# Splitting weights nearer to their use: merge by column chunks, the softmax projections' first weights loaded during the scans, the MLP's split moved inside its turn, the scans' tokens in quarters

## The reference, cut to what matters

```
h = rms_norm(x, norm_mix_g) * (1.0 + sc_m) + sh_m
proj = einsum('bsd,de->bse', h, w_in)            # a_q a_k a_v | b_* | c_* | gates (3 x 1024)
o_a = mixer_diff_attn(a_q, a_k, a_v, ...)        # softmax branch, 4 heads, width 512
o_b = mixer_hgrn2(b_*, ...)                      # gated scan, width 256
o_c = mixer_gla(c_*, ...)                        # gated scan, width 256
g_a, g_b, g_c = split(sigmoid(gates), 3)
merged = g_a * (o_a @ w_up_a) + g_b * (o_b @ w_up_b) + g_c * (o_c @ w_up_c)
x = x + gt_m * (merged @ w_out)
h = rms_norm(x, norm_mlp_g) * (1.0 + sc_f) + sh_f
x = x + gt_f * (square(relu(h @ mlp_w1)) @ mlp_w2)
```

## Time and profile before

| | |
|---|---|
| time, median of 3 runs | 4508.22 us (4507.63 to 4508.64) |
| the profiled execution | 4506.89 us |
| its span, first to last instruction | 4505.1 us |
| mean granted TensorE clock | 0.929 |
| PE busy | 3856.6 us (86%) |
| DVE busy | 2588.6 us (57%) |
| ACT busy | 1651.8 us (37%) |
| POOL busy | 502.5 us (11%) |

### The profile page before, as it was taken

The page is one execution under the profiler, slowest core; times in us unless marked ns, Lnnn a source line. Parts: engine busy times, 40 slices in busy tenths (PEclk is TensorE's granted clock), DMA queues, the critical chain, the costliest instruction groups (busy, mean ns, idle before and its releaser), DMA issues. The chain is left out here.

```text
span 4505.1 us, 56411 instructions
## 1 busy us (share of the span) xinstructions
PE 3856.6 (86%) x22256; PEld 3126.4 (69%) x22256; DVE 2588.6 (57%) x3973; ACT 1651.8 (37%) x2217; POOL 502.5 (11%) x471
## 2 busy tenths in 40 slices
PE   5988998977897999999797999499677798994996
PEld 2766876766676888886697887277566587872774
DVE  6266771159555555555433773587655465745776
ACT  2213331146330000003113773276613465732675
POOL 0001121000000000000131000034102000000341
PEclk9989999989898999999898999699888899996998
DMA  7101112230431111111213103299702302022998
GB/s 296 42 22 61 64 64 96 73 126 22 140 134 66 56 37 56 53 40 69 91 59 142 34 16 137 93 377 371 237 21 81 83 21 110 15 103 94 352 377 277
DMA packets 136489, 518.88 MB, mean 115 GB/s; under 512 B 17952, under 2 KB 70336, under 8 KB 118224
## 3 DMA queue, kind: packets, MB, share of 16 engines
q1 hardware_dynamic: 101936, 411.94, 24.9%
q0 software_dynamic: 31216, 101.85, 7.2%
q10 hardware_dynamic: 3120, 2.10, 0.2%
HBM read 427.21 MB, written 88.62 MB: 115 GB/s over the span
## 5 line engine op out<-in xcount | busy, mean ns | idle before, releaser
L2038 ACT ACTIVATE mlp_relu<-mlp_z 128x512 f32<-128x512 f32 x64 | 38.3, 598 | 641.1 <-PE mlp_z L155 641.1
L3083 DVE TENSOR_TENSOR ring_r<-ring,oN_r 128x4096 fp32r<-128x4096 f32 x48 | 212.2, 4424 | 67.4 <-ACT oN_r L3014 67.4
L153 PE MATMUL scans_G<-ring_r 128*128 128x512 f32 x544 | 221.8, 408 | 32.7 <-ACT scans_stg L2541 18.7
L3083 DVE TENSOR_TENSOR ring_r<-ring,hT_r 128x4096 fp32r<-128x4096 f32 x48 | 212.3, 4423 | 58.0 <-ACT hT_r L3014 58.0
L153 PE MATMUL mlp_z<-ring_r,mlp_w_high_r 128*128 128x512 f32 x512 | 201.3, 393 | 22.0 <-DVE ring_r L147 21.9
L3014 ACT ACTIVATE oN_r<-ring 128x4096 fp32r<-128x4096 f32 x48 | 174.0, 3628 | 84.1 <-DMA ring<-in_w_all 70.0
L154 PE MATMUL mlp_z<-hT_r,mlp_w_high_r 128*128 128x512 f32 x512 | 200.2, 391 | 0.0
L155 PE MATMUL mlp_z<-ring_r 128*128 128x512 f32 x512 | 200.2, 391 | 0.0
L153 PE MATMUL mlp_y_ps<-mlp_w_high_r,oN_r 128*128 128x512 f32 x512 | 199.6, 390 | 0.0
L155 PE MATMUL mlp_y_ps<-mlp_w_high_r,oN_r 128*128 128x512 f32 x512 | 199.2, 389 | 0.0
L154 PE MATMUL mlp_y_ps<-ring_r,oN_r 128*128 128x512 f32 x512 | 199.2, 389 | 0.0
(11 more groups left out here) (643 smaller groups left out, 10661.7 us busy)
## 6 DMA issues: line engine op xcount, KB each, us to landing
ring<-in_w_all SPq DMA_DIRECT2D x118, 2048.0 KB, 10.6
ring<-in_w_mlp SPq DMA_DIRECT2D x16, 2048.0 KB, 7.7
ring<-in_w_all SPq DMA_DIRECT2D x12, 1024.0 KB, 6.3
branch_gates<-scans_stg POOLq DMA_DIRECT2D x48, 256.0 KB, 2.3
merge_raw<-branch_gates SPq DMA_DIRECT2D x16, 768.0 KB, 5.1
ring<-in_w_even SPq DMA_DIRECT2D x6, 1536.0 KB, 8.2
qk_turned<-even_gemm_y POOLq DMA_DIRECT2D x48, 128.0 KB, 2.2
even_qk<-qk_turned SPq DMA_DIRECT2D x6, 1024.0 KB, 5.2
```

What stands on the lines that cost most here:

```text
L153: pe.matmul(out, lh, rh, start=start, stop=False)
L2038: act.activation(r[:, n % 2, :], Z[:, n % 4, :], ACT.Relu).then_inc(z_free, 1)
L3083: dve.tensor_tensor(buf_r[:, b, :], buf[:, b, :], w_high[n % RING].bitcast(F32), ALU.subtract)\
```

## The change

Four edits. In the merge, weights are cast and split by chunk (`ct`), one unit ahead of their use, and the token tiles 4 to 7 are turned, cast and split as 1, 1 and 2 tiles behind units 0, 1 and 2. The v weights of diff_gemm are loaded by SP in the scans, when the tiles of the last load but one are done, under a semaphore of their own (`v_in`), and are cast and split in two halves. The MLP's split of the next W1 follows the add for product 7 instead of 12. The tokens at the start of the scans are cast and split in quarters, and PE waits for quarters 0 and 1, and for 2 and 3.

```diff
@@ merge_stage
-        LATER = {0: (4, 5, 6, 7)}
+        LATER = {0: (4,), 1: (5,), 2: (6, 7)}
+        def chunk(t_, ct):
+            return t_[:, ct // 4, :].rearrange("p (k n) -> p k n", k=KD)[:, :, (ct % 4) * P:(ct % 4 + 1) * P]
 (PE)
-                if th == 0 and ct % 2 == 0:
-                    pe.wait_ge(w_split, half + 1)
+                if th == 0:
+                    pe.wait_ge(w_split, ct + 1)
 (ACT)
-            def cast(half):
-                act.wait_ge(m["up_in"][half], 16)
-                act.activation(w_high[:, half, :], buf[:, half, :], ACT.Copy).then_inc(w_cast, 1)
+            def cast(ct):
+                act.wait_ge(m["up_in"][ct // 4], 16)
+                act.activation(chunk(w_high, ct), chunk(buf, ct), ACT.Copy).then_inc(w_cast, 1)
             cast(0)
-            for t in range(NT):
+            for t in range(HT):
                 take(t)
-            cast(1)
             for g in range(N):
+                if g + 1 < KD:
+                    cast(g + 1)
+                for t in LATER.get(g - 1, ()):
+                    take(t)
 (DVE)
             low_w(0)
-            for t in range(NT):
+            for t in range(HT):
                 low_o(t)
             for g in range(N):
-                if g == 1:
-                    low_w(1)
+                if g + 1 < KD:
+                    low_w(g + 1)
+                for t in LATER.get(g - 1, ()):
+                    low_o(t)
@@ diff_gemm_stage
-            for s_ in range(NS):
+            for s_ in range(1, NS):
...
-                if s_ == 0:
-                    for h in range(4):
-                        sp.dma_start(kn(of(raw, 0))[:, :, h * P:(h + 1) * P], src[h, :, :, 2 * P:3 * P])\
-                          .then_inc(w_in[0], 16)
 (PE)
+                    if n == 0 and k % (KD // 2) == 0:
+                        pe.wait_ge(w_split, 1 + k // (KD // 2))
 (ACT)
-            cast_w(0)
+            act.wait_ge(m["v_in"], 64)
+            for part in range(2):
+                act.activation(half_of(high(0), part), half_of(of(raw, 0), part), ACT.Copy).then_inc(w_cast, 1)
@@ scans_stage (SP, behind the last of its loads)
+            sp.wait_ge(bg_done, last_tile(len(LOADS) - 2))
+            for h in range(4):
+                sp.dma_start(buf[:, 0, :].rearrange("p (k n) -> p k n", k=KD)[:, :, h * P:(h + 1) * P],
+                             m["w_diff"][h, :, :].rearrange("p (k n) -> p k n", k=KD)[:, :, 2 * P:3 * P])\
+                  .then_inc(m["v_in"], 16)
 (PE)
-                    pe.wait_ge(h_split, n + 1)
+                    pe.wait_ge(h_split, 2 * n + 2)
 (ACT; DVE alike)
-            def cast_h(half):
-                toks = slice(half * HALF, (half + 1) * HALF)
+            def cast_h(q):
+                toks = slice(q * 2 * P, (q + 1) * 2 * P)
             cast_h(0)
+            cast_h(1)
             cast_first(0, ready[first % RING], 16 * (first // RING + 1))
-            cast_h(1)
+            cast_h(2)
+            cast_h(3)
@@ mlp_stage (DVE)
-                    if n == NY - 4:
+                    if n == NT - 1:
                         dve.wait_ge(m["mlp_w_in"][0], i * 16 + 32)
                         split(step, dve, buf[:, 0, :], w_high[:, 0, :], buf_r[:, 0, :]).then_inc(w_split, 1)
```

More of the change, by code:

```diff
@@ L1388, in low_o, with low_w @@
                                   o_high[:, :, t * P:(t + 1) * P].bitcast(F32), ALU.subtract).then_inc(o_split, 1)
-            def low_w(half):
-                dve.wait_ge(w_cast, half + 1)
-                dve.tensor_tensor(buf_r[:, half, :], buf[:, half, :], w_high[:, half, :].bitcast(F32), ALU.subtract)\
+            def low_w(ct):
+                dve.wait_ge(w_cast, ct + 1)
+                dve.tensor_tensor(chunk(buf_r, ct), chunk(buf, ct), chunk(w_high, ct).bitcast(F32), ALU.subtract)\
                    .then_inc(w_split, 1)
             low_w(0)
-            for t in range(NT):
+            for t in range(HT):
                 low_o(t)
@@ L1440, in of, with half_of @@
             return slots[s_ % RING][:, 0:KD * WIDE[s_]]
+        def half_of(ap, part):
+            return ap[:, part * SLOT // 2:(part + 1) * SLOT // 2]
         def kn(ap):
@@ L1451, in _ @@
                     sp.wait_ge(done, LAST[s_ - RING])
-                if s_ == 0:
-                    for h in range(4):
-                        sp.dma_start(kn(of(raw, 0))[:, :, h * P:(h + 1) * P], src[h, :, :, 2 * P:3 * P])\
-                          .then_inc(w_in[0], 16)
-                else:
-                    sp.dma_start(kn(of(raw, s_)), src[s_ - 1, :, :, 0:2 * P]).then_inc(w_in[b], 16)
+                sp.dma_start(kn(of(raw, s_)), src[s_ - 1, :, :, 0:2 * P]).then_inc(w_in[b], 16)
         @block.gpsimd
@@ L1475, in _ @@
                 s_ = 0 if n < NT else 1 + (n - NT) // 4
-                if n == 0 or n in LAST:
-                    pe.wait_ge(w_split, s_ + 1)
+                if n in LAST:
+                    pe.wait_ge(w_split, s_ + 2)
                 if n >= 4:
@@ L1494, in cast_w @@
             def cast_w(s_):
-                act.wait_ge(w_in[s_ % RING], 64 if s_ == 0 else 16 + 64 * (s_ == 4))
+                act.wait_ge(w_in[s_ % RING], 16)
                 if s_ >= 2:
@@ L1513, in low_w @@
             def low_w(s_):
-                dve.wait_ge(w_cast, s_ + 1)
+                dve.wait_ge(w_cast, s_ + 2)
                 dve.tensor_tensor(of(low, s_), of(raw, s_), high(s_).bitcast(F32), ALU.subtract).then_inc(w_split, 1)
-            for s_ in range(NS):
+            for part in range(2):
+                dve.wait_ge(w_cast, part + 1)
+                dve.tensor_tensor(half_of(of(low, 0), part), half_of(of(raw, 0), part), half_of(high(0), part).bitcast(F32),
+                                  ALU.subtract).then_inc(w_split, 1)
+            for s_ in range(1, NS):
                 low_w(s_)
@@ L2646, in _, with low_h @@
             step = Steps(dve, stepped)
-            def low_h(half):
-                toks = slice(half * HALF, (half + 1) * HALF)
-                dve.wait_ge(h_cast, half + 1)
+            def low_h(q):
+                toks = slice(q * 2 * P, (q + 1) * 2 * P)
+                dve.wait_ge(h_cast, q + 1)
                 dve.tensor_tensor(h_low[:, :, toks], m["hT"][:, :, toks], h_high[:, :, toks].bitcast(F32), ALU.subtract)\
@@ L2658, in _ @@
             low_h(0)
+            low_h(1)
             low_first(0)
-            low_h(1)
+            low_h(2)
+            low_h(3)
             low_first(1)
@@ L3186, in build_program @@
         m["mlp_w_in"] = [ctx.enter_context(nc.semaphore(f"mlp_w_in{j}")) for j in range(2)]
+        m["v_in"] = ctx.enter_context(nc.semaphore("v_in"))
         m["up_in"] = [ctx.enter_context(nc.semaphore(f"up_in{j}")) for j in range(2)]
```

## The result

| | before | after |
|---|---|---|
| median beside each other, 4 runs each | 4507.93 us (4505.30 to 4508.64) | 4474.88 us (4470.33 to 4478.31) |
| ratio, 95% interval | | 0.9927 (0.9910 to 0.9944) |
| the profiled execution | 4506.89 us | 4474.20 us |
| its span | 4505.1 us | 4472.3 us |
| mean granted TensorE clock | 0.929 | 0.932 |

The change makes the kernel 33.1 us faster; 36.4 had been forecast. In two later comparisons the changed kernel was 38.8 and 40.6 us faster; the intervals of the three ratios overlap.

A forecast was written before the change was run, and what follows sets the result against it. TensorE, busy 86% of the span, was taken as the bound, with gains only from its gaps and slow clock; -13.5 - 20.9 - 1.9 - 0.1 = -36.4 gave 4470.5 profiled, 4471.8 us forecast as median, range 4465 to 4481.

The forecast's parts named there:

- v weights: Start of diff_gemm: weights loaded in the scans lie ready, PE starts at 781.4 instead of 794.90, -13.5 us.
- the halves alone: diff_gemm: if the load still came last, only half a cast and half a subtraction would be saved, -3.9 us.
- merge: start: Merge ahead of unit 0: tile 0 no longer waits for a whole slot's subtraction, -5.7 us.
- merge: unit 0: Merge's first unit: as slow as before, 13 matmuls in 5.64 us; 2.6 us more gained if the clock is up.
- merge: transposes: Merge behind unit 0: the four later tiles, spread, take 3.8 us instead of 5.39, -1.6 us.
- merge: waits, slow stretches: Merge: PE's waits for products go, -9.9 with 0.5 given back; slow stretches of 9 and 12 matmuls go, -4.2 us.
- tokens: Start of the scans: quarters hidden by ACT's wait for the weights' DMA, -0.1 us, between +0.5 and -0.5.
- (1): Merge: gates behind the feed overrun the 0.7 us slack, PE waits again, costing 6.1 us: 4477.9 us; 16%.
- (2): diff_gemm: early v load collides with stores or lands no sooner, -13.5 shrinks to -3.9: 4481.4 us; 3%.
- (3): Merge: the clock is up in unit 0 as well: 4469.2 us; 25%.
- (4): Merge: DVE reads 8-piece chunks slowly; sign turns from 5.7 us a chunk, 13.9 slower: 4522.1 us; 1%.
- (5): Merge: alternating casts and sigmoids on ACT load tables, 1.28 us twice a unit: 4475 us; 2%.

The follow-up runs named there:

- experiment 3: Kernel before with v weights cast and subtracted in halves, but loaded at diff_gemm's start as before: 4503.15 us, ratio 0.9981.
- experiment 5: Kernel before with only the tokens cast and split in quarters: 4505.11 us in one run.
- experiment 8: Kernel before with the ring's 4 MB feed issued behind the merge's second gate load instead of its third: 4506.89 us against 4506.40.
- experiments 1: Kernel before with the v weights' part alone, loaded in the scans and cast and subtracted in halves: 4494.57 us against 4509.16, ratio 0.9965.

## Why the prediction was right, step by step

| term | forecast | measured in the traces |
|---|---|---|
| v weights | -13.5 | -13.6 (794.90 to 781.32) |
| of it the halves alone | -3.9 (its terms add up to 3.84) | -3.5 (experiment 3) |
| merge: start | -5.7 | -5.8 (15.29 to 9.49) |
| merge: unit 0 | 0 (or -2.6) | -1.1 (8.32 to 7.22); -0.6 over 8 and 6 profiles |
| merge: transposes | -1.6 | -2.2 (5.39 to 3.24) |
| merge: waits, slow stretches | -9.4, -4.2 | -8.9, about -4 |
| merge in all | -20.9 | -22.6; -21.1 over 6 and 4 profiles |
| MLP | -1.9 | -2.2 |
| tokens | -0.1 | -0.2 here, -0.3 in experiment 5 |
| sum | -36.4 | -38.0 at the MLP's end, -36.1 over 2 and 3 profiles; -33.1, -38.8, -40.6 in the totals |

The mechanism was right in the merge, in diff_gemm and in the MLP; for the tokens it was not. There I had written that ACT's wait for the DMA hides them, while it was DVE that ended last, by 0.2 us. Four sizes were off besides. The transposes were priced at 0.96 us a tile, from a row that carries the modelled end of the last; from start to start a tile took 0.8 in the changed kernel. Unit 0's clock was taken as unchanged; it stood at 0.76 on average instead of falling to half at once, as it does in some profiles of the old merge too. A chunk was priced as a quarter of a slot, 0.9 and 1.1 us; it took 1.04 on ACT and 1.22 on DVE, since an instruction's fixed part is not divided. And the slow stretches were taken from one profile. Where the prediction lets unit 3 start at 1161.7, the number is that of unit 4, which is the one whose second product waits; the slack that follows from it is right.

The merge in the first profile of before was also slower than usual: 128.1 us, where five others with the old merge had 125.8 to 127.0. The waits are nearly the same in them; what differs is how many matmuls behind each wait are slow. Behind the wait of 3.69 us the window of the earlier trace rows has 12 matmuls in 5.20 us; the same window has 16 in the second profile of before, and 23, at full clock, in experiment 3, one fence each:

```profile
1180.40:1185.60 5.20, 5.20 (x16) 4.12 (x17) 4.82 (x7) 1.16 (x1) 0.00 (x0) 0.67 0.19 42
```

```profile
1181.82:1187.02 5.20, 5.20 (x23) 4.31 (x24) 4.81 (x7) 1.16 (x1) 0.00 (x0) 1.00 0.21 41
```

In the six profiles with the old merge and the late feed, the waits were 3.55 to 3.69 us, and 12, 8, 8, 7, 0 and 0 matmuls behind them ran at the slow rate. So the term of 2.4 for this stretch is the upper end of what such a wait leaves behind, and nothing is the lower. That the forecast of the merge met the mean of the profiles so closely, -20.9 against -21.1, is in part luck: this term was high, and the transposes and unit 0 low.

**The rivals.** (1) The gates still came behind the feed, 17.2 us, as it said, but the slack held. What it left is the 0.5 us for chunk 5. By the Trainium skill, "DMA: Bandwidth & Descriptors", section "Queues, rings and completion order", descriptors of one queue on one DMA engine start in order; the trace of before agrees, with 3.9 MB moved between the gates' issue and their landing. With the feed issued earlier (experiment 8), the longest landing fell from 9.7 to 7.1 us and the wait went. (2) The early load did all that it says (experiments 1 and 3). (3) The clock was up in unit 0 for the first 6 matmuls, then 7 were slow. (4) Chunks cost DVE 1.23 us instead of 1.11, far from the 5.7 at which the sign would have turned. (5) There was one table load in the merge, at 1119.62, and casts and sigmoids alternated without another.

What the prediction did not have is the scatter of the stages behind. It took one profile's 1.3 us to the median as all the uncertainty of the kernel before; the same code behind the MLP varies by 14 us between profiles. The total of the first comparison, 4474.88, is 3.1 above the forecast. In the profiled pair the 5.0 us given back behind the MLP account for that; for the other runs, which were not profiled, it is the likely reason and not shown. Why those stages scatter stays open; among them are those in which the page has the DMA engines busy nine tenths or more of a slice, at 352 to 377 GB/s in the pages of before and after, but no run here varied that.

## What to carry to other kernels

When a wait for an engine's result is removed, ask first what stands in that engine's queue ahead of the result: here moving casts behind the first sigmoid brought about 13 us of the merge's 21, the finer pieces 5 and the spread tiles 3. Split a weight only as far as the path from its arrival to the first matmul needs it, and issue its load where its buffer comes free, even in the stage before. Price an edit by the marks of its own stage, and take two profiles of the kernel before ahead of explaining a few microseconds of the total.

## What the runs showed of the hardware

Behind the same wait of 3.55 to 3.69 us in the merge the granted clock stayed low for 12 matmuls in one execution, for 7 or 8 in three and for none in two; a wait's price in clock is a range, here 0 to 2.4 us. In the changed kernel the clock did not fall at the end of a 2.37 us wait but 1.6 us behind it, 1121.6 against 1119.97; in the first profile of before the first matmuls behind the same wait were slow already. A subtraction over 8 pieces of 128 columns took DVE 1.23 us, what the contiguous ones of 512 to 4096 elements a partition give for its 1024, so here the pieces cost nothing. A single instruction costs 0.15 us (DVE) or 0.19 us (ACT) and then 1.04 or 0.84 ns an element, by casts of 0.61, 1.91 and 3.62 us and subtractions of 0.69, 2.29 and 4.42 us for 512, 2048 and 4096. In a row they cost less of it: eight casts of 512 took 4.27 us where two halves took 3.71, and eight subtractions 4.91 where two took 4.49, 0.09 and 0.07 us for each further one.
